# Expert gates of tokens 128 to 255: from one-hot matmuls to an accumulating indirect scatter through device memory

## The reference, cut to what matters

```python
def chunk(xi):
    q = (xi @ w_query).reshape(B, PEER_CHUNK, PEER_HEADS, 2, PEER_HALF)
    s = jnp.einsum('bthpd,hpnd->bthpn', q, sub_keys)
    s1, i1 = lax.top_k(s[..., 0, :], PEER_TOPK)
    s2, i2 = lax.top_k(s[..., 1, :], PEER_TOPK)
    cand = (s1[..., :, None] + s2[..., None, :]).reshape(B, PEER_CHUNK, PEER_HEADS, PEER_TOPK * PEER_TOPK)
    top_s, top_c = lax.top_k(cand, PEER_TOPK)
    idx = (jnp.take_along_axis(i1, top_c // PEER_TOPK, axis=-1) * PEER_N_KEYS
           + jnp.take_along_axis(i2, top_c % PEER_TOPK, axis=-1))
    g = jax.nn.softmax(top_s.astype(jnp.float32), axis=-1)
    u = jnp.take(expert_down, idx, axis=0)
    act = jax.nn.gelu(jnp.einsum('btd,bthkd->bthk', xi, u).astype(jnp.float32))
    v_sel = jnp.take(expert_up, idx, axis=0)
    return jnp.einsum('bthk,bthkd->btd', (g * act).astype(xi.dtype), v_sel)
```

## Time and profile before

| | us |
|---|---|
| median of 3 runs (lowest, highest) | 2108.61 (2107.28, 2109.04) |
| span of the profiled execution, first to last instruction | 2104.1 |
| what lies around it, taken as median less span | 4.5 |
| TensorE busy / VectorE / ScalarE / GpSimd | 2080.3 / 1454.7 / 1274.4 / 365.7 |

### The profile page before, as it was taken

One profiled execution on the slowest core, in us unless ns is written; L12 is line 12 of the kernel. 1 busy time (PEld: TensorE's weight loads), 2 busy tenths in 40 slices (PEclk: granted clock), 3 DMA queues, 4 the chain that ended last, 5 costly groups with the idle time before them and its releaser, 6 DMA issues.

```text
span 2104.1 us, 32329 instructions
## 1 busy us (share of the span) xinstructions
PE 2080.3 (99%) x12464; PEld 1806.7 (86%) x12464; DVE 1454.7 (69%) x2582; ACT 1274.4 (61%) x2171; POOL 365.7 (17%) x177
## 2 busy tenths in 40 slices
PE   8999999999999999999999999999999999999998
PEld 7889988888888888887899888888888888788997
DVE  7969988889865555567589888898555555533346
ACT  6664588877644444465645888877544444544564
POOL 1457700000000000012477000000000000154231
PEclk9999999999999999999999999999999999999999
DMA  6455555555566666664456555555666666856344
GB/s 226 151 160 171 175 177 170 164 175 166 168 196 194 193 194 194 194 202 137 136 169 183 174 164 173 168 170 171 190 191 195 194 191 197 268 181 194 106 141 130
DMA packets 105468, 373.16 MB, mean 177 GB/s; under 512 B 12205, under 2 KB 15685, under 8 KB 104933
## 3 DMA queue, kind: packets, MB, share of 16 engines
q1 hardware_dynamic: 105316, 371.11, 58.0%
HBM read 369.97 MB, written 1.10 MB: 176 GB/s over the span
## 4 chain that ended last, share of the span: by engine, by line
PE 95%; DVE 3%; DMA 1%; ACT 1%; issue 0%; POOL 0%; SPq 0%; DVEq 0%; ACTq 0%
PE ps L184 22%; PE ps L178 18%; PE ps L180 17%; PE ps L179 17%; PE ps L185 11%; PE ps L1039 3%; PE ps L1018 1%; DMA raw<-in_w_qk_dram 1%; PE ps L1062 1%; DVE WL L166 1%; PE ps L2141 1%; PE ps L2168 0%; PE ps L2149 0%; DVE arena L754 0%; PE ps L1065 0%
## 5 line engine op out<-in xcount | busy, mean ns | idle before, releaser
L161 ACT ACTIVATE WH<-raw 128x1024 fp32r<-128x1024 f32 x680 | 717.6, 1057 | 483.6 <-PE ps L180 416.0
L166 DVE TENSOR_TENSOR WL<-raw,WH 128x1024 fp32r<-128x1024 f32 x554 | 680.5, 1230 | 71.7 <-ACT WH L161 71.2
L184 PE MATMUL ps<-X,WH 128*128 128x512 f32 x2016 | 716.0, 399 | 2.3 <-DVE WL L166 2.2
L171 POOL TENSOR_TENSOR WL<-raw,WH 128x1024 fp32r<-128x1024 f32 x126 | 314.5, 2500 | 1620.6 <-ACT WH L161 1619.8
L185 PE MATMUL ps<-X,WL 128*128 128x256 f32 x2016 | 563.1, 279 | 0.0
L184 PEld LDWEIGHTS ps<-X,WH 128*128 128x128 f32 x2016 | 378.6, 188 | 89.4 <-DVE WL L166 2.7
L185 PEld LDWEIGHTS ps<-X,WL 128*128 128x128 f32 x2016 | 380.7, 189 | 0.1
L178 PE MATMUL ps<-WH,X 128*128 128x512 f32 x960 | 378.5, 394 | 2.1 <-DVE X L365 0.9
L180 PE MATMUL ps<-WH,X 128*128 128x512 f32 x960 | 374.2, 390 | 0.0
L179 PE MATMUL ps<-WL,X 128*128 128x512 f32 x960 | 374.0, 390 | 0.0
L178 PEld LDWEIGHTS ps<-WH,X 128*128 128x128 f32 x960 | 180.4, 188 | 42.1 <-issue 2.5
(11 more groups left out here) (307 smaller groups left out, 2335.6 us busy)
## 6 DMA issues: line engine op xcount, KB each, us to landing
raw<-in_l_down_dram SPq DMA_DIRECT2D x256, 512.0 KB, 3.7
raw<-in_l_up_dram SPq DMA_DIRECT2D x256, 512.0 KB, 4.2
raw<-in_l_wq_dram SPq DMA_DIRECT2D x32, 512.0 KB, 3.7
raw<-in_w_qk_dram SPq DMA_DIRECT2D x24, 512.0 KB, 4.0
raw<-in_w_gates_dram SPq DMA_DIRECT2D x24, 512.0 KB, 3.7
raw<-in_l_nat_dram SPq DMA_DIRECT2D x16, 512.0 KB, 3.5
raw<-in_l_wout_dram SPq DMA_DIRECT2D x16, 512.0 KB, 3.7
raw<-in_l_win_dram SPq DMA_DIRECT2D x16, 512.0 KB, 4.4
```

The source lines that it names most:

```text
L161: a.activation(WH[:, i % NW, :], raw[:, i % NW, :], ACT.Copy).then_inc(w_high, 1)
L166: v.tensor_tensor(WL[:, i % NW, :], raw[:, i % NW, :], WH[:, i % NW, :], ALU.subtract).then_inc(w_low_v, 1)
L171: g.tensor_tensor(WL[:, i % NW, :], raw[:, i % NW, :], WH[:, i % NW, :], ALU.subtract).then_inc(w_low_g, 1)
L184: t.matmul(PS[:, bank, :], w[0], X2[:, k, :, :].rearrange("p w t -> p (w t)"), start=first, stop=False)
```

## The change

Tokens 0 to 127 keep the one-hot products: `GROUPS` goes from 32 to 16, `turn_picked` transposes 3 blocks and not 6, and the tables have 128 columns and not 256. At most 128 tokens are open from then on.

Tokens 128 to 255 go another way. Two tables of 8 MB in device memory (`spread`, one for each layer) are zeroed by 16 writes of 512 KB each from a zeroed buffer `BLANK`; SyncE issues those of layer 0 between the loads 12 to 57, those of layer 1 between the loads of layer 0's up stage. VectorE computes the target address of each pick (`SPOT`) and its gate (`SENT`). GpSimd then issues 128 indirect transfers per layer, each with one 4-byte element from each of 128 partitions (one pick of each of the 128 tokens), which add to the table; ahead of every 16th it waits for all issued so far. Just after load up-2, SyncE waits for all 128 and for the last product group. From there on it reads the table back, 256 KB for two pairs of chunks, between the up loads, and GpSimd multiplies each pair's late half of `G` by it, before ScalarE rounds that pair.

Several semaphores are merged, so that some waits now cover more transfers than before (`pos_in` waits for 4 transfers and not 2).

```diff
-        SPREAD, PACE, GROUPS = 25, 3, 32
+        SPREAD, PACE, GROUPS = 25, 3, 16
...
+        BLANKS = ({12 + 3 * n: n for n in range(16)}, {P0 + 148 + 6 * n: n for n in range(16)})
+
+        def blank(s, l, i):
+
+            if i not in BLANKS[l]:
+                return
+            n = BLANKS[l][i]
+            if n == 0:
+                s.wait_ge(blank_up, l + 1)
+            s.dma_start(spread[l][:, 1024 * n:1024 * n + 1024], BLANK).then_inc(blank_out, 16)
+
+        def load_late(s, l, p):
+
+            if p == 0:
+                s.wait_ge(gate_add, 2048 * l + 2048)
+                s.wait_ge(prod, GROUPS * l + GROUPS)
+            if p >= 4:
+                s.wait_ge(late_up, 64 * l + p - 2)
+            s.dma_start(LATE[:, p % 4:p % 4 + 2].rearrange("p a j t -> p (a j t)"),
+                        spread[l][:, 256 * p:256 * p + 512]).then_inc(late_in[p // 2 % 2], 16)
+
         def peer_sync(s, l):
             wq, down, up = bases(l)
             for i in range(wq + 4, up + 128 + 4):
                 load(s, i)
+                blank(s, 0, i)
+                if l == 0:
+                    blank(s, 1, i)
+                p, r = divmod(i - up + 2, 2)
+                if r == 0 and p % 2 == 0 and 0 <= p < 64:
+                    load_late(s, l, p)
...
-            for tt in range(2):
-                for i in range(3):
-                    m = t.transpose(PS[:, 4 + tt, i * 128:i * 128 + 128], TK[:, tt, i, :], ident)
+            for i in range(3):
+                m = t.transpose(PS[:, 4, i * 128:i * 128 + 128], TK[:, 0, i, :], ident)
...
+            a.wait_ge(late_up, 64 * l + p + 1)
             a.activation(gh, G[:, 2 * p:2 * p + 2, :].rearrange("p e t -> p (e t)"), ACT.Copy).then_inc(g_high, 1)
...
-            for t in range(2):
-                m = v.tensor_tensor(gt[:, t], gt[:, t], SM[:, 8 + 8 * t:16 + 8 * t].unsqueeze(2).to_broadcast([128, 8, 16]),
-                                    ALU.mult)
-            m.then_inc(tk_up, 1)
+            sent = SENT[:, :].rearrange("p (h k) -> p h k", k=16)
+            v.scalar_tensor_tensor(out=TW[:, 1, :], in0=TK[:, 1, 1, :], scalar=128.0, in1=TK[:, 1, 0, :], op0=ALU.mult,
+                                   op1=ALU.add).then_inc(vec.sem, vec.up())
+            v.tensor_tensor(gt[:, 0], gt[:, 0], SM[:, 8:16].unsqueeze(2).to_broadcast([128, 8, 16]),
+                            ALU.mult).then_inc(tk_up, 1)
+            v.tensor_tensor(sent, gt[:, 1], SM[:, 16:24].unsqueeze(2).to_broadcast([128, 8, 16]),
+                            ALU.mult).then_inc(vec.sem, vec.up())
+            v.wait_ge(vec.sem, vec.n - 1)
+            v.tensor_scalar(SPOT[:, :], TW[:, 1, :], 128.0, SM[:, 120:121], ALU.mult, ALU.add).then_inc(vec.sem, vec.up())
...
         def mixer0_gpsimd(g):
+            g.memset(BLANK, 0.0).then_inc(blank_up, 1)
...
         def onehots(v, l, s):
+            if s == 0:
+                v.wait_ge(blank_out, 256 * (l + 1))
...
         def peer_gpsimd(g, l):
             wq, down, up = bases(l)
-            for c in range(272):
+            for c in range(44):
+                low_g(g, wq + c + 2)
+            g.wait_ge(blank_out, 256 * (l + 1))
+            g.wait_ge(it_up, l + 1)
+            everywhere = bass.AP(spread[l], 0, [[1, 128 * 16384], [1, 1]])
+            for j in range(128):
+                if j and j % 16 == 0:
+                    g.wait_ge(gate_add, 2048 * l + 16 * j)
+                g.indirect_dma_start(out=everywhere, out_offset=bass.IndirectOffsetOnAxis(ap=SPOT[:, j:j + 1], axis=0),
+                                     in_=SENT[:, j:j + 1], in_offset=None, compute_op=ALU.add).then_inc(gate_add, 16)
+            if l == 0:
+                g.wait_ge(prod, GROUPS)
+                g.memset(BLANK, 0.0).then_inc(blank_up, 1)
+            for p in range(64):
+                late = G[:, 2 * p:2 * p + 2, 128:256]
+                g.wait_ge(act_tail, N_TAIL * l + TAILS[2 * p + 1])
+                g.wait_ge(late_in[p // 2 % 2], 16 * (16 * l + p // 4 + 1))
+                g.tensor_tensor(late, late, LATE[:, p % 4], ALU.mult).then_inc(late_up, 1)
+            for c in range(270, 272):
                 low_g(g, wq + c + 2)
```

More of the change, by code:

```diff
@@ L100, in build @@
         GH, GL_ = sb("GH", [128, 512], F32R)[:, :], sb("GL", [128, 512], F32R)[:, :]
+        with nc.sbuf_tensor("LATE", [128, 8, 2, 128], F32) as LATE:
+            pass
+        BLANK = LATE[:, 4:8, :, :].rearrange("p a j t -> p (a j t)")
         Y2 = sb("Y2", [128, 4, 2, 256], F32R)
@@ L112, in build @@
         scr = nc.dram_tensor("scr_rel", [24, 512], F32, kind="Internal")
+        spread = [nc.dram_tensor(f"gates_by_expert{l}", [128, 16384], F32, kind="Internal") for l in range(2)]
         ident = CST[:, C_ID:C_ID + 128]
@@ L142, in build @@
         acc, x_add = sem("acc_done"), sem("x_added")
-        rel_in, rel_out = sem("rel_in"), sem("rel_out")
+        rel_out = sem("rel_out")
         trig_up = sem("trig_up")
+        blank_up, blank_out, gate_add = sem("blank_up"), sem("blank_out"), sem("gates_added")
+        late_in, late_up = [sem(f"late_in{i}") for i in range(2)], sem("late_gated")
         def load(s, i):
@@ L724, in mixer0_vector @@
             L = PVT[:, PV_LB:PV_LB + 12].rearrange("p (r h) -> p r h", r=3)
+            v.tensor_tensor(PLACE, ident, iota, ALU.mult).then_inc(vec.sem, vec.up())
+            v.wait_ge(vec.sem, vec.n)
+            v.tensor_reduce(SM[:, 120:121], PLACE, AX, ALU.add).then_inc(vec.sem, vec.up())
             m, lb, oml = LB[:, 0, :], LB[:, 4, :], LB[:, 5, :]
@@ L1350, in select_pairs @@
             v.wait_ge(vec.sem, vec.n)
-            for t in range(2):
-                m = v.tensor_tensor(gt[:, t], gt[:, t], SM[:, 8 + 8 * t:16 + 8 * t].unsqueeze(2).to_broadcast([128, 8, 16]),
-                                    ALU.mult)
-            m.then_inc(tk_up, 1)
+            sent = SENT[:, :].rearrange("p (h k) -> p h k", k=16)
[7 more added lines that the diff above has]
+            v.tensor_scalar(SPOT[:, :], TW[:, 1, :], 128.0, SM[:, 120:121], ALU.mult, ALU.add).then_inc(vec.sem, vec.up())
         def picked_tables(v, l):
[L1359 to L1362, removed]
+            ps = PS[:, 4, 0:384].rearrange("p (i t) -> p i t", i=3)
+            gate, sig = TK[:, 0, 2, :], TK[:, 0, 0, :]
+            high, low = GATE0, [GP16[:, k, :] for k in range(2)]
             v.wait_ge(tk_T, l + 1)
             for i in range(2):
-                v.tensor_copy(IB[:, i, :].rearrange(half, a=2), ps[:, i]).then_inc(vec.sem, vec.up())
+                v.tensor_copy(IB[:, i, :], ps[:, i]).then_inc(vec.sem, vec.up())
             v.tensor_scalar(gate.bitcast(U32), ps[:, 2].bitcast(U32), 0x7F800000, None,
@@ L1370, in picked_tables @@
             v.wait_ge(vec.sem, vec.n)
-            v.tensor_copy(EXP2.rearrange(half, a=2), gate).then_inc(vec.sem, vec.up())
+            v.tensor_copy(EXP2, gate).then_inc(vec.sem, vec.up())
             v.tensor_copy(low[0], sig).then_inc(vec.sem, vec.up())
@@ L2111, in block2_sync @@
             s.wait_ge(b_mm, STEPS)
-            s.dma_start(FG, d["rows"][0:1, RW_FG:RW_FG + 1024].to_broadcast([128, 1024])).then_inc(fg_in, 16)
+            s.dma_start(FG, d["rows"][0:1, RW_FG:RW_FG + 1024].to_broadcast([128, 1024])).then_inc(last_in, 16)
             for i in range(G0 + 19, END):
```

104 lines of the change are left out of this document (53 added, 51 removed).

## The result

The changed kernel takes 2300.72 us in the median of 4 runs (2294.23 to 2306.79) against 2108.34 before; the ratio is 1.0913, with a 95% interval of 1.0900 to 1.0927. I had forecast 2079.1 and a range of 2073 to 2120. The time lies far above it, on the side that the rival "scatter late" described with 2227.

A forecast was written before the change was run, and what follows sets the result against it. TensorE, busy 99% of the span, was taken to bound the kernel; 28.8 us of gate groups and 0.7 of transposes saved, all else at nothing: 2108.6 - 29.5 = 2079.1 us, range 2073 to 2120.

The forecast's parts named there:

- scatter late: Turn to up: GpSimd's issue, waits included, over 2.30 us a transfer; SyncE stands at up-2; time 2227 at 2.6; chance 0.15.
- TensorE's gain: Gate groups: 32 fewer at 0.90 us, 28.8 us, plus 0.7 for fewer transposes; sum 29.5 us.
- the tables: VectorE around the halved gate tables: instructions replaced or moved, 2.47 us wait anyway; cost nothing, otherwise 1 us a layer.
- the added traffic: Table reads and zeros beside the weight loads: up stage of layer 0 at 254 GB/s, share about 0.85; cost nothing.
- the late half: Up stage: 64 GpSimd products of 0.65 us, 42 us of 347, and 32 SyncE reads; cost nothing.
- up stage short of DMA: Rival: layer 0's up loads pushed past 8.2 us by the 16 writes, 1 us each; time 2095; chance 0.09.
- The time that the scatter has: From the tables to SyncE's wait after up-2: 280 us plus 14.1 leeway, 294 us, 2.30 for each transfer.
- The issue: GpSimd's issue of one indirect transfer: 1.6 us, two to three times SyncE's, for 128 transfers.
- The seven landings: GpSimd's seven real waits for a landing in the scatter: 3.7 to 6.5 us each, 35 us in all.
- Within 16 nothing waits for a landing: Scatter: reason for pricing transfers near the issue row; 128 x 1.6 + 35 = 240 us against 294, cost nothing.
- My upper bound: Scatter, each transfer landing before the next is issued: 128 x 6.5 = 832 us, costing 1076 us.
- GpSimd blocked by VectorE: Rival: scatter issues wait for running VectorE instructions, 2.17 us each, 313 us a layer; time 2117; chance 0.08.

The follow-up runs named there:

- noscatter: The changed kernel without the 128 indirect transfers of each layer and the wait for them; table still zeroed, read back and multiplied in: 2078.01 us (ratio 0.9858).
- none: The changed kernel without zeroing, indirect transfers, table reads, GpSimd's late products and the waits on them: 2077.42 us (ratio 0.9857).
- fit4352: The changed kernel with 4352 bytes of room for GpSimd's transfers, not 1024, gate tables and scatter lists moved into parts of `G`: 2103.82 us (ratio 0.9986).
- ring2048: The changed kernel with 2048 bytes of room for GpSimd's transfers, not 1024, all else the same: 2155.04 us (ratio 1.0214).
- plain: The changed kernel, still with 1024 bytes, its indirect transfers writing and not adding: 2077.92 us (ratio 0.9857).

## Why the prediction was wrong, step by step

- *TensorE's gain* (29.5 us): right; against 2107.38, the kernel before in the same job, `noscatter` saves 29.4 us and `none` 30.0. 512 matmuls are left on the gate line, 35.0 us.

```profile
L1079 PE MATMUL ps<-ONE 128*128 128x128 f16 x512 | 35.0, 219 | 0.0
```

- *The other engines, the tables, block 0, the added traffic, the late half*, each costed at nothing: right. The last two are 0.6 us between two medians, inside the spread, and the gain of `none` leaves nothing for the others. GpSimd's product takes 0.87 us in the mean, not 0.65, and this is hidden too. The rival "up stage short of DMA" falls with it: TensorE is busy 100.00 of 100 us at 249 GB/s.
- *The time that the scatter has* (294 us, 2.30 each): nearly right. SyncE's waits cost somewhat less than they last. The profiled execution of `fit4352` took 2101.4 us, 23.4 above the 2078.0 of `noscatter`, with waits of 42.0; that of `ring2048` 2158.2, 80.2 above with 97.1; that of the changed kernel 2306.8, 228.8 above with 248.6. So 8 to 10 us of each layer's wait are free in these three, where I had 14.1, and the scatter had about 290 us.
- *The issue* (1.6 us): right, 1.70; the 0.30 between two issues was missing, up to 38 us a layer. *The seven landings* (35 us): they took 19. With issue, 0.30 and seven waits alone, 128 x 2.0 + 7 x 3 = 277, the scatter would have fitted, as that of `plain` did with 259.5.
- *"Within 16 nothing waits for a landing"*: this is the step that failed. I took an issue as the only price and let the transfers queue without bound. The 1024 bytes stood in the kernel's text and I did not ask what they hold. With 1024 bytes, 51 more pauses arise in a layer, some 140 us, and the 240 us of my sum became 398.4. My upper bound, a landing for each transfer, covered this; I gave the way to it too little weight, since nothing in the trace of before showed a limit.
- *Rival "scatter late"*: right in place (up-2), in the waits that would show it and in its price, 2 x (128t - 294) with t = 398.4 / 128 = 3.11, which gives 208 beside the measured 222.7; layer 1's scatter took 408.1, and with both layers the formula gives 218.5. Its cause was different: GpSimd was not slow in issuing but stood between issues.
- *Rival "GpSimd blocked by VectorE"*: small. In the gap, when VectorE is idle, issues take 1.55 to 1.57 us; over the layer the mean is 1.70. That is 0.15 x 128 = 19 us a layer with VectorE and the loads together, not separated here, where I had allowed 0.57 each.

## What to carry to other kernels

A transfer issued by GpSimd has a price for its issue and a second one that comes every so many issues, set by the room for its transfers: run the transfer alone at two or three sizes of that room and read the beat (an adding one used it up about twice as fast as a plain one here) before the room is shrunk to make space for a tile. More room is not always better, as 5056 bytes against 4608 show; the beat should fall together with the waits that the kernel needs anyway, and only the places of the pauses in the trace show where it falls. When a new wait is put into the queue that feeds all engines, compare the pace of what it waits for with the pace needed, here 2.30 us a transfer, with a margin of more than the unknowns in it.

## What the runs showed of the hardware that I had not expected

- GpSimd's pauses at fixed counts of its own transfers, independent of how many are still under way: 3.28 us ahead of the 19th issue at 5056 bytes, with two transfers out. The count runs on from one scatter to the next, at all eight sizes.
- A size of 4608 bytes is faster than 5056 by 31.3 us and than 4352 by 20.7 us, in the same program.
- 128 single floats added to device memory cost the issuing engine 1.56 us at the median, and 0.97 when only written, but cost the stream of 512 KB loads beside them nothing that could be measured (2076.6 to 2078.0 us).
